# Where the quadrant sums of the unsummed tiles stand, which tiles get their sums ahead, and how three kinds of deferred steps are spaced, in a two-layer decoder step

## The reference, cut to what matters

```
for i in (0, 1):                                   # two layers, D_MODEL 1024, D_FF 2816
    x = x + 0.5 * swiglu(rmsnorm(x, norm_ffn[i, 0]), w_gate_up[i, 0], w_down[i, 0])
    h = rmsnorm(x, norm_mix[i])
    x = x + (even_mixer(h) if i == 0 else odd_mixer(h))
    x = x + 0.5 * swiglu(rmsnorm(x, norm_ffn[i, 1]), w_gate_up[i, 1], w_down[i, 1])
    gate = sigmoid(rmsnorm(x, norm_ple[i]) @ w_ple_gate[i])
    emb  = rmsnorm(p[i] @ w_ple_proj[i], norm_ple_proj[i])
    x = x + gate * emb
y = rmsnorm(x, norm_final)
# swiglu(h, Wgu, Wd) = (silu(h @ Wgu[:, :D_FF]) * (h @ Wgu[:, D_FF:])) @ Wd
```

## Time and profile before

| what | value |
|---|---|
| median of 3 runs (lowest, highest) | 2517.54 us (2515.68, 2533.95) |
| the profiled execution | 2516.08 us, span of its slowest core (core 2) 2514.5 us |
| spans of the 8 cores | 2491.2 to 2514.5 us |
| busy on core 2: PE, DVE, ACT, POOL | 96%, 71%, 40%, 33% of the span |
| matmuls on core 2 | 13470 |

### The profile page before, as it was taken

How to read it: one execution, slowest core, us unless ns; L and a number is a source line. 1 busy time by engine, 2 the same in 40 slices (tenths; PEclk the granted TensorE clock), 3 DMA queues, 4 the chain that set the end, 5 groups by cost and what they waited for, 6 DMA issues and landing times.

```text
span 2514.5 us, 36235 instructions; the slowest of 8 cores (2491.2 to 2514.5 us)
## 1 busy us (share of the span) xinstructions
PE 2411.8 (96%) x13470; PEld 1155.0 (46%) x13470; DVE 1785.7 (71%) x2939; ACT 999.5 (40%) x1757; POOL 826.8 (33%) x885
## 2 busy tenths in 40 slices
PE   7899999999999889999999999999999999999996
PEld 3343455545444335554444445554444444455442
DVE  5868675866677586568887667577687877664887
ACT  3234432435752334144561434243333514432354
POOL 1344854211321735440021745433165214300000
PEclk9888999999999999999999999999999999999998
DMA  7697578654446878875047968865361467434323
GB/s 145 163 232 199 120 196 248 180 111 102 116 123 182 199 208 230 251 225 122 1 138 200 226 189 237 248 188 94 54 141 42 141 181 205 156 117 153 111 48 131
DMA packets 109905, 399.39 MB, mean 159 GB/s; under 512 B 13680, under 2 KB 47088, under 8 KB 101408
## 3 DMA queue, kind: packets, MB, share of 16 engines
q1 hardware_dynamic: 72000, 292.79, 34.4%
q0 software_dynamic: 37008, 103.17, 25.5%
q10 hardware_dynamic: 720, 1.11, 0.2%
HBM read 359.14 MB, written 124.39 MB: 192 GB/s over the span
## 4 chain that ended last, share of the span: by engine, by line
PE 77%; DVE 13%; DMA 3%; ACT 3%; issue 3%; POOL 1%; ACTq 0%; DVEq 0%; POOLq 0%; SPq 0%
PE ps L617 77%; DVE x L587 3%; DMA ringh<-wts 2%; DVE hh L587 2%; DVE ringh L580 2%; DVE hih L580 1%; DVE scr L580 1%; DVE scr L587 1%; DVE h L587 1%; ACT scr L574 1%; POOL ringh L583 1%; ACT L572 1%; DVE ht L580 1%; DVE hit L580 1%; ACT sq L574 1%
## 5 line engine op out<-in xcount | busy, mean ns | idle before, releaser
L617 PE MATMUL ps<-hh,ringh 128*128 128x512 f16 (+1 forms) x3856 | 719.2, 338 | 1.4 <-DMA ringh<-wts 1.0
L574 ACT ACTIVATE scr<-ps 128x512 f32<-128x512 f32 (+1 forms) x819 | 440.6, 544 | 657.6 <-PE ps L617 637.3
L617 PE MATMUL ps<-ht,ringh 128*128 128x512 f16 x2016 | 480.9, 386 | 21.9 <-DVE scr L580 10.7
L617 PEld LDWEIGHTS ps<-hh,ringh 128*128 128x128 f16 x3856 | 338.7, 99 | 341.2 <-issue 31.8
L580 DVE TENSOR_TENSOR scr<-ps,scr 128x512 f32<-128x512 f32 x524 | 356.6, 687 | 172.1 <-PE ps L617 161.2
L617 PE MATMUL ps<-h,ring 128*128 128x512 bf16 (+1 forms) x2420 | 462.9, 347 | 7.8 <-DVE scr L587 3.9
L587 DVE SCALAR_TENSOR_TENSOR x<-ps,x 128x512 f32<-128x512 f32 (+1 forms) x512 | 318.8, 638 | 193.3 <-PE ps L617 192.6
L580 DVE TENSOR_TENSOR hih<-ps,scr 128x512 f16<-128x512 f32 x352 | 242.8, 690 | 162.8 <-PE ps L617 146.6
L617 PE MATMUL ps<-hih,ringh 128*128 128x512 f16 x1408 | 333.7, 385 | 1.0 <-DVE x L587 1.0
L617 PEld LDWEIGHTS ps<-h,ring 128*128 128x128 bf16 x2420 | 216.5, 98 | 239.1 <-ACT scr L574 4.9
L617 PEld LDWEIGHTS ps<-ht,ringh 128*128 128x128 f16 x2016 | 197.5, 99 | 272.6 <-issue 24.2
(11 more groups left out here) (122 smaller groups left out, 1834.0 us busy)
## 6 DMA issues: line engine op xcount, KB each, us to landing
ringh<-wsum SPq DMA_DIRECT2D x115, 896.0 KB, 6.7
wsum<-ringh SPq DMA_DIRECT2D x45, 896.0 KB, 6.1
ringh<-wts POOLq DMA_DIRECT2D x61, 512.0 KB, 8.7
wsum<-stgn SPq DMA_DIRECT2D x32, 896.0 KB, 6.4
ringh<-wsum SPq DMA_DIRECT2D x22, 1120.0 KB, 6.8
ringh<-wsum SPq DMA_DIRECT2D x17, 1344.0 KB, 9.2
wsum<-ringh SPq DMA_DIRECT2D x15, 1344.0 KB, 8.0
stgn<-wts POOLq DMA_DIRECT2D x32, 512.0 KB, 7.2
```

What stands on the lines that cost most here:

```text
L574: return e.activation(out=out, in_=in_, func=func, **kw)
L617: ins = e.matmul(o_, l, r, start=st, stop=sp, skip_group_check=cont)
```

## The change

It has five edits. (1) The list `EARLY`: every second slice is presummed (0, 1, then 2, 4, ... 20), then down tiles dn(1, 0), dn(1, 1), then gu 3 and gu 11, then the rest; before it was 0 to 6 in a row, then 8, 10, 12, 14. (2) The first SwiGLU's presum starts 34 us of the plan after pass 1 begins, not 50; it stops at 165 us either way. (3) The twelve sums of hidden slices leave the `tail` of the raw tiles. T14 of j = 2 to 5 is called in `gu_quad` of slice j + 6, just ahead of its T23. The six sums of j = 0, 1 and 6, 7 are deferred from the end of `gu_first`, from 9 us of the plan on, 1.5 us apart, and flushed ahead of the down tiles. All twelve stay on DVE. (4) `emb_stats` of b2, b3 and SB starts 5, 14 and 20 us of the plan later, not 0.6 us each. (5) The final norms of b0 and b1 in the last layer have their eight operations 2.2 us of the plan apart, not 0.7.

```diff
-    EARLY = [("gu", m) for m in (0, 1, 2, 3, 4, 5, 6, 8, 10, 12, 14)] + [("dn", 1, 0), ("dn", 1, 1)]
-    EARLY += [("gu", m) for m in (16, 18, 20)] + [("dn", 1, 2), ("dn", 1, 3), ("dn", 0, 0), ("dn", 0, 1)]
-    EARLY += [("gu", m) for m in range(21, 6, -2)]
+    EARLY = [("gu", m) for m in [0, 1] + list(range(2, 22, 2))] + [("dn", 1, 0), ("dn", 1, 1), ("gu", 3), ("gu", 11)]
+    EARLY += [("dn", 1, 2), ("dn", 1, 3), ("dn", 0, 0), ("dn", 0, 1)] + [("gu", m) for m in range(21, 4, -2) if m != 11]
...
-    def emb_stats(l, b):
+    def emb_stats(l, b, wait=0.6):
...
-        defer(0.6, s0, tag)
+        defer(wait, s0, tag)
...
+    before = {}
...
         if j >= h:
+            before.pop(j, lambda: None)()
             hid_T23(j - h, j)
...
                 sfree(sg)
-                if b == 1:
-                    if j >= h:
-                        hid_T23(j - h, j)
-                    hid_T14(j, h)
             defer(3.7, tail, ("tail",))
...
         ensure(("tail",))
+        for j in range(NRAW - h, h):
+            before[j + h] = lambda j=j: hid_T14(j, h)
+        for j in range(NRAW - h):
+            fs = (lambda j=j: hid_T14(j, h), lambda j=j: hid_T23(j, j + h), lambda j=j: hid_T14(j + h, h))
+            for i, f in enumerate(fs):
+                defer(9.0 + 6.0 * j + 1.5 * i, f, ("rt",))
...
-                    t0 = 0.0 if l or f else 50.0
+                    t0 = 0.0 if l or f else 34.0
                     at_time(pe_t[0] + t0, lambda: W.presum("norm", nl, nf, 11.5, 10.5, 1.3, "sp", 165.0 - t0), ("next",))
...
+                ensure(("rt",))
                 keys = [("dn", l, f, pi, q, p) for q in range(4)]
...
                 if emb:
-                    for b in PAIRS[1] + (SB,):
-                        emb_stats(l, b)
+                    for b, wait in zip(PAIRS[1] + (SB,), (5.0, 14.0, 20.0)):
+                        emb_stats(l, b, wait)
...
-                nm[b] = Norm(b, gnext, "pe", {2: 2.2, SB: 1.0}.get(b) if l else 2.5 if b > 1 else 1.6)
+                nm[b] = Norm(b, gnext, "pe", {0: 2.2, 1: 2.2, 2: 2.2, SB: 1.0}.get(b) if l else 2.5 if b > 1 else 1.6)
```

## The result

The changed kernel takes 2561.24 us (median; 2553.42 to 2769.53) where the kernel before takes 2516.80 beside it: 1.0162 of it, 95% interval 1.0122 to 1.0203. The forecast was 2497, so it missed by 64 us and by sign. Executions in which a whole die has a lower mean clock than the other and a longer span, as in that of 2769.53 us, with cores 4 to 7 at 0.88, are left out of every comparison here.

The account below looks back on a forecast made before the run. PE was taken to set the end. Core 7, then slowest, was to gain 6.8 + 5 + 1.2 + 1.0 + 3.4 = 17.4 us, from 2512.4 to 2495.0; with measurement offsets 2497 us was predicted, range 2484 to 2514 (8 in 10).

Parts of the forecast that it names:

- What bounds the kernel: Whole kernel: PE sets the end, busy 218.5 of 220 us over 280 to 500 us; gains where it waits carry through.
- Sums of the raw tiles: End of the raw tiles: without the sums PE's wait goes, 7.8 us, 1.0 comes back; net gain 6.8, 3 to 8.
- I keep all of it: Transfers of 100 to 260 us: they start earlier too, so the raw tiles' net 6.8 us passes them whole.
- By turns: Part two of pass 0: alternating presummed slices spare POOL; second SwiGLU gains 5 (core 7) or 10 us (core 2), third 1.2.
- all 4.5 us on core 7 go, all 10.0 on core 2: Second SwiGLU, part two of pass 0: these PE losses vanish entirely; taken as 5 and 10 us of gain.
- Just covered; 0: Start of pass 0, raw slices 3 and 5: 14.3 us of loading fits within 15.6; cost 0, up to 1.5 a pass.
- Embedding statistics: Both ple layers: moving the statistics later relieves a small stall; 1.0 us gain, from -3 to +2.
- about three more: ple: three spaced reciprocal roots add about three table loads, 3.9 us of ACT, hidden unless DVE has no slack.
- Final norms: Last ple, b2 and SB: wider spacing recovers half of 6.8 us PE idle; gain 3.4 us (1 to 5.5).
- Presum at 34 us: First SwiGLU's pass 1: an earlier presum start costs 0, up to 1 us.
- the gains are only put off: Rival, chance 0.15: DVE falls behind in slices 8 to 11, raw slices 3 and 5 arrive late; 2507 us.
- the clock stretch moves: Rival, chance 0.12: the 0.81 stretch comes 60 us or more later, over pass 1; 2520, or 2527 us.

Follow-up runs that it names:

- norm_only: The kernel before with only the final norms of b0 and b1 at 2.2 us; 1.0015 of the kernel before.
- raw_norm: The kernel before with only the raw tiles' sums moved and the final norms spaced; 1.0001 (0.9968, 1.0034) in a many-stretch session.
- turns_early: The kernel before with the new list, the presum from 34 us, and a summed down tile's store put off 2.0 us, not 3.5; 1.0074 (1.0038, 1.0111).
- before_here: The kernel before, unchanged, profiled again on a chip where other experiments ran; run for its stages alone, no whole time given.

## Why the prediction was wrong

- **What bounds the kernel: right.** PE sets the end, and losses pass on: 12.2 us on cores with no stretch, for about 10 of waits by the stages.
- **Sums of the raw tiles: mechanism right, net gain mis-sized; the step that failed is "I keep all of it".** PE's wait went and 7 to 8 us with it, for 7.8. But the transfers of 100 to 260 us did not start early enough: PE waits for landings at the first down tiles, 3.38 and 3.28 us on one core, and 3 to 6 us come back in place of 1.0. Forecast 6.8 net; measured 2.3 alone, and 5.3 together with the norms where the clock takes nothing, so some 3.
- **By turns: the step that failed is "all 4.5 us on core 7 go, all 10.0 on core 2".** It counted POOL's cycles only. A presummed tile's load moves to SP's queue, there in front of q3's store, and this costs POOL 13.99 us and PE 5.0: +6.1 in slices 12 to 15, and the old wait stays behind it. "Just covered; 0" for raw tiles 3 and 5 was right on landings; PE waits for DVE there instead, 1.9 and 2.5 us, shown in the fourth SwiGLU beside POOL's sums. The third SwiGLU gives 0.6 to 0.9 of its 1.2. Term: -6.2 forecast, some +7 measured.
- **Embedding statistics: the step that failed is "about three more" loads, hidden by ACT.** There are eight more a layer, by the estimate 0.45 us of PE each, and DVE's backlog at the moved work costs the rest: 1.0 of gain forecast, from 3 of loss to 2 of gain; measured a loss of 5.2 and 6.0 at b0 and b1 of the two layers, less 1.3 that each gives back with b2 and SB, 8.6 in all and 10.9 in the mean of cores. It is the largest error that the diff names. "ACT is busy 21 of 39" was an average; the loads are a chain in which each tanh waits.
- **Final norms: mechanism right, size off.** b2 and SB give 2.8 for 3.4, and 0.8 comes back with b3: 2 in their stages, and nothing that norm_only's whole time shows.
- **Presum at 34 us:** nothing in the stages points to it, but it was never run by itself.
- **The rival "the gains are only put off"** had a part of the truth: the raw tiles' gain does come back, though by landings and not by DVE, and raw slices 3 and 5 cost about what it gave them.
- **The clock: the rival "the clock stretch moves" came true**, given 0.12; the forecast left the stretch where it was, at no cost, and that is the other step that failed. The starts at 174 to 218 us lie in the rival's "60 us or more later". Its price, 23 to 30 us, was too high for one stretch (20.3 by the spans, for 9.1 before, so 11 more), and it didn't have the second. That the start follows a return of the clock from 0.50 is seen each time and not shown as a cause. All eight cores run dense (PE is busy 95 to 97% of the first 2500 us on each in before, the changed kernel and raw_norm), PE is at 1.00 between the stretches in every session, but for the drops to 0.50, and the long stretches come by pairs of cores.

In sum: 17.4 of gain forecast. By waits it is 3 of gain for the raw tiles, 7 of loss for the turns, 8 or 9 for the embedding, 2 of gain for the norms, so some 10 of loss; the other 19 of the stages' 29 lie where the stretches lie, and more on the slowest core, which is one with two stretches. A small slip stands in the forecast's last step: 2495.0 with the 1.6 and the 1.5 that it names is 2498, not 2497.

## What to carry to other kernels

Before moving a transfer to another engine's queue, write down what stands behind it there and which buffer its own wait needs: a store that frees a slot should be ahead of a load that waits for one (7.0 us of loss in slices 12 to 15 went to 0.0 by it). Before spacing out steps that need another activation table, count the changes in the order that results, with everything that is pending there, not only the steps moved; a bunch ahead of the tanh was nearly free (4 loads, PE busy 41.5 of 41.9 us, where 12 loads went with 42.3 of 47.3). After taking a stall away, look at what PE waits for next: here about half of the gain went, 3 to 6 of 7 us, first of all to weights that had not landed. And where long slow-clock stretches occur, each began 3.2 to 10.3 us after the clock's return from 0.50 behind idle time of PE on at least one core of the pair: list the stalls that are left or new, and cost the change once with a stretch behind each.

## What the runs showed of the hardware

- The granted clock has three values in the twenty profiles: 0.50, 0.81 and 1.00. A drop to 0.50 lasts 3.4 to 10.2 us (327 in the six profiles with long stretches), with at least 1.7 us of PE idle in the 10 us ahead.
- A long stretch of 0.81 comes to a pair of cores at once, lasts 158 to 163 us (sixteen of them in those six), and began 3.2 to 10.3 us after the granted clock's return from 0.50 to 1.00 on 30 of 32 cores. In other sessions there are 63 to 114 stretches a core, 15.2 us long or 7 to 9 in the median, and the same kernel takes 6% longer, 2667 to 2670 us for 2516; in others again almost none (2512 to 2513 us).
- A long stretch costs a core 9.1 us in the kernel before, where nearly all lie ahead of pass 1, and 20.3 in the changed kernel, where they reach into it; the two means are from different sessions.
- A table load is 1.28 us with the next activation 0.01 us behind it; six of them with three small roots cost PE 2.7 us, 0.45 each, where PE is busy 41.5 of 41.9 us and ACT 22.9.
- A store of 1344 KB took 13.1 us (core 3 of the changed kernel) when two loads were issued within 0.7 us ahead of it, and 9.5 (core 3 of turns_early) when the nearest was 1.3 us ahead.
- Three DVE operations of 512 columns took 3.46 us beside POOL's sums (core 1 of turns_early) and 1.67 without (core 1 of before_here).
